# Odd mixer: index products and score products of two heads issued together, each over its own 64 rows

## The reference

```python
logit_idx = einsum('bqhd,bkd->bqhk', q_idx, k_idx) * 64 ** -0.5          # 8 heads, depth 64
score = einsum('bqh,bqhk->bqk', w, relu(logit_idx))                      # then causal, top 64 keys
s = einsum('bqhl,bqkl->bqhk', q_lat, c_sel) * 64 ** -0.5 + bias          # 16 heads
p = softmax(s);  o = einsum('bqhk,bqkl->bqhl', p, c_sel)
```

## Time and profile before

| what | value |
|---|---|
| time of the profiled execution | 1470.55 us |
| its span in the trace | 1468.8 us |
| median of three other runs | 1471.29 us (1470.66 to 1471.62) |
| PE busy | 1434.4 us, 98% of the span |
| VectorE busy | 958.8 us, 65% |
| ScalarE busy | 698.5 us, 48% |
| granted TensorE clock, mean | 0.998 of full speed |
| odd mixer in the trace | about 1145 to 1250 us |

### The profile page before, as it was taken

How to read it: one execution, slowest core, us unless ns; L and a number is a source line. 1 busy time by engine, 2 the same in 40 slices (tenths; PEclk the granted TensorE clock), 3 DMA queues, 4 the chain that set the end, 5 groups by cost and what they waited for, 6 DMA issues and landing times. The chain is left out here.

```text
span 1468.8 us, 26041 instructions
## 1 busy us (share of the span) xinstructions
PE 1434.4 (98%) x10266; PEld 1320.2 (90%) x10266; DVE 958.8 (65%) x1559; ACT 698.5 (48%) x1119; POOL 86.2 (6%) x140
## 2 busy tenths in 40 slices
PE   8999999999999999999999999999999999999998
PEld 7887998899998999989989999999999878899997
DVE  4765657766667766667467666676665667576665
ACT  6753444544345434456564434353443656544342
POOL 1040001000002000010000000000000114000000
PEclk9999999999999999999999999999999999999999
DMA  9343001655553645524336545545555423365440
GB/s 348 145 152 130 1 1 44 240 201 189 176 204 127 224 171 195 191 90 169 128 113 244 203 171 198 189 158 190 200 182 183 162 86 144 145 217 196 171 172 29
DMA packets 26575, 238.06 MB, mean 162 GB/s; under 512 B 2544, under 2 KB 6784, under 8 KB 7808
## 3 DMA queue, kind: packets, MB, share of 16 engines
q1 hardware_dynamic: 23824, 233.39, 43.5%
q10 hardware_dynamic: 2672, 3.58, 0.7%
HBM read 235.89 MB, written 1.07 MB: 161 GB/s over the span
## 5 line engine op out<-in xcount | busy, mean ns | idle before, releaser
L440 PE MATMUL ps<-uT_h,w_gu 128*128 128x256 f32 x3520 | 614.0, 280 | 0.3 <-DVE w_gu L1952 0.2
L440 PEld LDWEIGHTS ps<-uT_h,w_gu 128*128 128x128 f32 x3520 | 537.7, 188 | 11.0 <-issue 1.4
L440 PE MATMUL ps<-uT_l,w_gu 128*128 128x256 f32 x1760 | 478.7, 279 | 0.0
L440 PE MATMUL ps<-w_dn,h_r 128*128 128x512 f32 x1320 | 326.2, 396 | 0.3 <-DVE h_r L1994 0.3
L440 PEld LDWEIGHTS ps<-uT_l,w_gu 128*128 128x128 f32 x1760 | 325.4, 188 | 0.0
L440 PEld LDWEIGHTS ps<-w_dn,h_r 128*128 128x128 f32 x1320 | 239.4, 188 | 51.2 <-issue 1.7
L1302 ACT CAST w_gu<-ring 128x2048 fp32r<-128x2048 f32 x110 | 209.9, 1909 | 155.1 <-PE ps L440 154.7
L1952 DVE TENSOR_TENSOR w_gu<-ring,w_gu 128x2048 fp32r<-128x2048 f32 x110 | 252.1, 2292 | 34.4 <-ACT w_gu L1302 34.0
L1985 DVE TENSOR_TENSOR us<-ps,bc 128x256 f32<-128x256 f32 x110 | 46.5, 423 | 202.4 <-PE ps L440 202.4
L1315 ACT ACTIVATE wk<-wk 128x256 f32<-128x256 f32 x110 | 46.2, 420 | 261.5 <-DVE wk L1983 261.4
L1308 ACT CAST w_dn<-ring 128x1024 fp32r<-128x1024 f32 x110 | 115.7, 1052 | 82.8 <-PE ps L440 82.6
(11 more groups left out here) (385 smaller groups left out, 1804.2 us busy)
## 6 DMA issues: line engine op xcount, KB each, us to landing
ring<-wstream SPq DMA_DIRECT2D x144, 1536.0 KB, 6.2
cst<-consts_in SPq DMA_DIRECT2D x1, 2185.0 KB, 13.8
wk<-t_row ACTq DMA_DIRECT2D x1, 2048.0 KB, 7.9
wk<-masks_in SPq DMA_DIRECT2D x1, 1216.0 KB, 24.2
x<-x_in SPq DMA_DIRECT2D x2, 512.0 KB, 4.9
ring<-wstream SPq DMA_DIRECT2D x1, 1024.0 KB, 9.0
inh<-gains ACTq DMA_DIRECT2D x2, 512.0 KB, 9.2
out_dram<-x SPq DMA_DIRECT2D x3, 256.0 KB, 2.1
```

The source lines that it names most:

```text
L440: return pe.matmul(o, l, r, start=start, stop=stop, skip_group_check=True)
```

## The change

What it does: where a head's operands lie on 64 rows, the product uses only those rows; and the products of the two heads of a block are issued one behind the other, the first into bank 0 and the second into bank 1. Index products come as pairs ahead of passes k = 1 and k = 5 of q0 to q3, and a pair waits for both relus of the pair before. Scores of units i and i + 1 are issued in step i where i is even, after max_ready of unit i - 1; odd steps issue no score. Order and waits on the other engines stay as they are.

```diff
--- before.py
+++ after.py
@@ -273,7 +273,8 @@
                             dist=fbias[t][:, h, :]))
                 if kind == "dsa":
                     for h in range(16):
-                        units.append(dict(q=oqT[:, h // 2, tk], k=khT[h % 2][:, h // 2, 0:K], K=K, scale=1.0,
+                        r = slice(h % 2 * HD, (h % 2 + 1) * HD)
+                        units.append(dict(q=oqT[r, h // 2, tk], k=khT[h % 2][r, h // 2, 0:K], K=K, scale=1.0,
                                           v=[vh[kt][:, h * HD:(h + 1) * HD] for kt in range(t + 1)],
                                           t5=bias16[:, h, P * (1 - t):P * (1 - t) + K], sel=selm[:, t, 0:K]))
             return units
@@ -1011,9 +1012,12 @@
                     if i == 0:
                         pe.wait_ge(s["idx_relu"], 16)
                         pe.wait_ge(s["c_ev"], 1)
-                    if i >= 2:
-                        pe.wait_ge(s["max_ready"], u - 1)
-                    mm(ps[i % 2][:, 0:a["K"]], a["q"], a["k"]).then_inc(s["S_ps"], 1)
+                    if i % 2 == 0:
+                        if i:
+                            pe.wait_ge(s["max_ready"], u)
+                        for m in range(2):
+                            d = units[i + m]
+                            mm(ps[m][:, 0:d["K"]], d["q"], d["k"]).then_inc(s["S_ps"], 1)
                 lag = 3 if i <= LAG_FROM else 4
                 if i >= 3 and i != LAG_FROM + 1:
                     u, a = b + i - lag, units[i - lag]
@@ -1121,13 +1125,15 @@
 
                 def idx(m):
 
-                    t, h = m // 8, m % 8
+                    t, c = m // 8, m % 8 // 2
                     if m >= 2:
-                        pe.wait_ge(s["idx_relu"], m - 1)
+                        pe.wait_ge(s["idx_relu"], m)
                     if m == 0:
                         pe.wait_ge(s["item_ev"], IB["odd"] + ODD_ITEMS.index(("qi", 3)) + 1)
-                    mm(ps[m % 2][:, 0:P * (t + 1)], qiT[:, h // 2, t * P:(t + 1) * P],
-                       kiT[:, h % 2, 0:P * (t + 1)]).then_inc(s["idx_ps"], 1)
+                    for h in range(2):
+                        r = slice(HD * h, HD * (h + 1))
+                        mm(ps[h][:, 0:P * (t + 1)], qiT[r, c, t * P:(t + 1) * P],
+                           kiT[r, h, 0:P * (t + 1)]).then_inc(s["idx_ps"], 1)
 
                 for n, it in enumerate(ODD_ITEMS):
                     q = IB["odd"] + n
@@ -1140,7 +1146,7 @@
                     elif it[0] == "q":
                         blk = 4 + it[1]
                         if it[1] < 4:
-                            steps = {1 + 2 * i: (lambda m=4 * it[1] + i: idx(m)) for i in range(4)}
+                            steps = {1 + 4 * i: (lambda m=4 * it[1] + 2 * i: idx(m)) for i in range(2)}
                         else:
                             steps = {2 + 2 * i: (lambda st=st: dsa(st)) for i, st in enumerate(DSA_STEPS[it[1]][:-1])}
                         last = col_split("odd", bank, 3 + blk, between=steps)
```

## The result

| | before | after |
|---|---|---|
| median of 20 runs each | 1470.96 us | 1472.86 us |
| profiled execution's span | 1468.8 us | 1471.1 us |
| PE busy | 1434.4 us | 1435.1 us |

The medians differ by +1.90 us (0.13%); the ratio, which goes by means, is 1.0023 with an interval of 1.0014 to 1.0031. It lies above the difference of the medians because 3 of the 20 runs after took 1477.2, 1484.5 and 1486.0 us, at a mean granted clock of 0.995, 0.989 and 0.989 where the others had 0.998 or 0.999; without them the median of the change is 1472.82. In a second session the change took 1472.87 against 1471.13.

A forecast was written before the change was run, and what follows sets the result against it. TensorE, busy 98%, was taken as the bound, other engines pacing q4 to q7 and steps 14 to 21 at places. Terms 0.43 + 0 + 0.74 + 0.40 + 0.07 + 0.07 gave +1.7 us: 1473.0, range 1470.4 to 1475.8.

The forecast's parts named there:

- the bounds: Whole kernel: switch price +-0.8 us, q4 -0.3 to +0.1, stalls in steps 16 to 31 from -0.6 to +1.2; 0 to +3.8.
- The price of a pair: Around each pair: 0.40 us for both row switches; 0.61 narrow and 0.83 wide, so +0.19 and -0.03.
- Index: q0 to q3: four narrow and four wide pairs, +0.18, +0.37 and -0.12, in sum +0.43 us.
- q4 to q7: Scores there: q4 0 (between -0.3 and +0.1), q5 and q6 +0.37 us each, q7 +0.40.
- Steps 14 to 21: Chain through three engines starts 0.40 us late from q7; step 22 then reached another +0.07 later.
- Steps 22 to 29: Wide step pairs 2.07 us instead of 2.10, four at -0.03, plus a 0.3 stall; +0.18.
- The stall ahead of pair 26: Behind step 23, where DVE has `piece`, the new wait's 0.2 us cover is gone: a stall of 0.3.
- The end: Steps 30 to 35: emptying the pipe no longer waits for the last score, -0.1 us.
- The waits as a whole: New relu and maximum waits: nothing in q2, q3 (at most a tenth or two); 0.3 us ahead of pair 26.
- a wash of switches and halved streams: The forecast's own case, over all pairs: switch costs about offset halved streaming, +1.7 us; chance 75%.
- The rival of the free switch: All index and score pairs: switching costs nothing, each pair saves half; 5.5 us less, 1465.8; chance 6%.
- The rival of the waits: max_ready ahead of pairs 16 to 30: the pair's wait becomes the bound, adding 4 us, 1477; chance 16%.

The follow-up runs named there:

- single products over 64 rows: Kernel before with its order, banks and waits, but each index and score product one at a time over its head's own 64 rows: 1485.37 against 1471.01 us.
- groups of eight: Kernel before with all eight index products of a query block over 64 rows in one stay, relus waiting for the group: 1468.12 against 1471.00 us.
- pairs over 128 rows: Order, banks and waits of the change, but each index and score product over all 128 rows as before: 1472.55 against 1471.01 us before.
- score half: Kernel before with only the score edits of the change, index products as before: 1472.70 against 1471.01 us.
- later piece: The change with DVE's first output piece behind step 19 instead of 18: 1472.54 against 1471.00 us before; again, 1473.44 against the change's 1472.87.
- wide fours: Kernel before with the 16 wide scores over 64 rows in groups of four, maxima waiting for the whole group: 1471.02 against 1471.00 us.
- these and the eights: Kernel before with both index products in eights and wide scores in fours over 64 rows: 1468.66 against 1471.00 us.
- index pairs: Kernel before with only the index edits of the change, scores as before: 1471.36 against 1471.01 us.
- both kernels with eight index products and full scores: Kernel before with index products in eights, first output piece behind step 18 or 19: 1468.12 against 1471.00 us, and 1468.84 against 1471.13 us.

## Why the prediction was right

It was forecast 1473.0 us, within 0.2% of before; the median is 1472.86, or +1.90 where +1.7 stood. The low and high ends of the range, 1470.4 and 1475.8, are wider than the bounds that they are put down to: 1471.29 and 0 to +3.8 give 1471.3 to 1475.1. The median lies inside of both.

*The price of a pair* carried the forecast, and it holds to 0.01 us: 0.61 and 0.83. It was read off the neighbours of `gla_A` and `rwkv_A`, not from the records of the products themselves, which show only the overlap. The single products over 64 rows and the groups of eight show it from both sides: the same 0.40 for one product, for two and for eight (0.43 and 0.41 around the eights). With the rule that a change of tiling mode drains the engine (the Trainium skill, TensorEngine Tiling (Array Packing), Key Properties) the runs agree: 0.20 us an edge. The factor of up to 2 of the same page, Theoretical Speedup, holds for the streaming only; a pair keeps none of it.

*Index*: +0.47 where +0.43 stood. The last wide pair waited for 0.2 ("a tenth or two"), on relus that DVE holds back.

*q4 to q7*: 0.02 to 0.06 off each. The first transpose came 0.2 late, and the fourth score behind the item, 0.3 with its start from idle, was gone, as worked out; the value product now has that start instead, 0.1.

*Steps 14 to 21*: q7's 0.40 through ScalarE's output weights and DVE came as said, with DVE's part at 1229.58, 1.94 later as all the rest there; then +0.07, measured +0.07: the last transposes of step 21 start at 1238.11 against 1236.10, 2.01 later, less the 1.94. This stretch hardly depends on the price of a pair: in the pairs over 128 rows, where q7 itself costs less, q7 to step 21 came out at +0.39 against the +0.44 here. The idle 0.91 ahead of pair 20/21 takes the place of the 0.69 on the result.

*Steps 22 to 29*: the step pair of 2.07 is exact. The stall ahead of pair 26 was put at 0.3 and is 0.1.

*The end* is the term that failed: "emptying the pipe no longer waits for the last score: -0.1". It was +0.29. The score of unit 31 does come earlier, with its partner at the head of step 30. But both scores now stand ahead of step 30's transposes, and ScalarE copies these before it can do exponential 30, the output piece's cast and exponential 31. Before:

```profile
1245.99 0.39 PE L1034 MATMUL ps<-cst,inh 128*128 128x128 f32 x2
...
1246.41 0.37 ACT L1601 COPY inh<-ps 128x256 f32<-128x256 f32 x1 [0.54 <-PE ps L1034]
```

After:

```profile
1248.39 0.39 PE L1038 MATMUL ps<-cst,inh 128*128 128x128 f32 x2
...
1248.82 0.37 ACT L1607 COPY inh<-ps 128x256 f32<-128x256 f32 x1 [0.95 <-PE ps L1038]
...
1249.59 0.58 ACT L1540 CAST uT_h<-ps 128x512 fp32r<-128x512 f32 x1
1250.05 0.52 ACT L1599 ACTIVATE inh<-inh,small 128x256 f32<-128x256 f32 x1
...
1250.71 0.44 PE L1038 MATMUL ps<-cst,inh 128*128 128x128 f32 x2
```

At the piece ahead of step 30 the trace was 1.97 us behind (1.49 and the 0.48), at these transposes 2.40, at their copy 2.41, and at the last transposes 2.22 (1248.49 before). An error of 0.4 us here and one of 0.2 with the opposite sign in steps 22 to 29 partly cancelled: that the sum came within 0.1 of the trace is in part luck.

*The waits as a whole* were right in sum for the change and too low as a mechanism: the pairs over 128 rows show that order and waits cost 1.5 us without any change of rows. Beside that kernel the change loses 1.25 us in q0, q1 and from q4 to step 21, where the narrow pairs are, and gets back 0.59 in q2 and q3 and 0.51 from step 22 on. In q2 and q3 the reason can be read: in both kernels the last wide pair starts 0.05 or 0.06 us after the end of the relu it waits for, but from there to the next pass it takes 0.73 in the change and 0.97 in pairs over 128 rows, since only the stream, now halved, and the way back are left to pay; going over falls into the wait. So "a wash of switches and halved streams" leaves out the waits. How much of the +1.9 belongs to which can't be said by subtraction, because a wait begins where the stream ahead of it ends.

The rival of the free switch (5.5 us less) is excluded by every run. The rival of the waits, at +4 beyond the forecast, did not come about: of pairs 16 to 30 two stood idle for DVE (16 for 0.27, 20 for 0.91), and pair 26 came 0.1 late.

## What to carry to other kernels

In this kernel products over half of the rows that are issued two by two really ran at once, but look at what stands ahead of and behind them: each stay on 64 rows cost 0.40 us here, so one pair of 128 columns loses, one of 256 breaks even, and eight in one stay save 0.4 to 1.3 us. Collect them, and let the readers wait for the group. And where two buffers are filled together, both readers must be done before the next fill: the slack of a double buffer is gone; and what stands behind a group in its step comes later by the whole group, which counts where a pipeline empties.

## What the runs showed that was not expected

The granted clock. In every kernel with score products over 64 rows some executions ran at a mean clock below 0.998: 5 of 31 of the change, 5 of 11 of the score half, 5 of 22 with the later piece, 1 of 11 with the wide fours, 2 of 11 with these and the eights, 2 of 6 of the single products (those two took 1506 us). In the kernel before, the index pairs, the pairs over 128 rows, and both kernels with eight index products and full scores, none did, in 132 runs. Against the pairs over 128 rows alone this is weak: with 5 of 31 in the change, 11 runs without a fall can be chance. Stretches of the first profiled execution with the later piece, columns as in the earlier trace rows:

```profile
1225.00:1230.00 5.00, 3.93 (x32) 3.28 (x30) 2.48 (x5) 3.42 (x11) 2.41 (x2) 1.00 0.29 79
...
1232.00:1234.00 2.00, 1.65 (x8) 1.22 (x6) 0.87 (x4) 1.03 (x4) 1.40 (x3) 0.50 1.06 449
```

and of the single products:

```profile
1235.00:1238.00 3.00, 2.67 (x18) 2.02 (x17) 0.69 (x4) 2.01 (x5) 1.25 (x2) 1.00 0.39 78
...
1240.00:1285.00 45.00, 45.00 (x145) 29.84 (x146) 14.41 (x48) 13.73 (x46) 9.68 (x14) 0.50 0.20 84
...
1287.00:1292.00 5.00, 5.00 (x26) 4.05 (x25) 0.00 (x0) 0.06 (x1) 0.00 (x0) 1.00 0.00 0
```

The clock falls from 2.4 to 1.2 GHz in the steps that stand alone, behind q7, where TensorE works over 64 rows for part of the time and also stands idle at places: it had been busy for 3.93 of 5.00 us ahead of the first fall and for 2.67 of 3.00 ahead of the second. In the single products it then stayed at 1.2 GHz for 45 us in which TensorE counted as busy all the time, and came back only in the output projection. The kernel before is not free of falls either: its profiled execution has a short one far ahead of the mixer, behind a stretch in which it was busy for 3.21 of 4.00 us:

```profile
234.00:236.00 2.00, 2.00 (x12) 2.00 (x10) 1.90 (x5) 0.00 (x0) 0.00 (x0) 0.50 0.03 8
```

What sets off the falls in the mixer was not tried by itself and stays open; the runs show only in which kernels they came. It matters for the choice: score products over 64 rows come with some runs that are 1 to 14 us longer than the others of their kernel (22 in the single products), which is one more reason to leave the scores as they were and keep the groups of eight.
